# Both parts of a norm's operand at one place modulo 512 bytes

## The reference, cut to what matters

```python
def first_block(x, p, w_in, ...):
    for i in range(DEPTH):
        h = mixer_block(h, norm_mix[i], w_in[i], ...)   # rmsnorm(h) @ w_in, retention, gated delta rule
        u = rmsnorm(h, norm_ffn[i])
        if i % 2 == 0:
            h = h + swiglu(u, ffn_w_gate[j], ffn_w_up[j], ffn_w_down[j])
        else:
            h = h + moe(u, router[j], exp_w_gate[j], exp_w_up[j], exp_w_down[j])
        h = h + jax.nn.sigmoid(rmsnorm(h, norm_ple[i]) @ w_ple_gate[i]) * (p[i] @ w_ple[i])

def second_block(x, norm1_g, w_in, ...):
    for l in range(DEPTH):
        h = rmsnorm_2(x, norm1_g[l])
        u = jnp.einsum('btd,de->bte', h, w_in[l])       # then mLSTM, attention and HGRN side by side
        x = x + jnp.einsum('bte,ed->btd', mix, w_out[l])
        a = jnp.square(jax.nn.relu(jnp.einsum('btd,df->btf', rmsnorm_2(x, norm2_g[l]), w_up[l])))
        x = x + jnp.einsum('btf,fd->btd', a, w_down[l])
```

## Time and profile before

| | |
|---|---|
| median of three runs | 2189.08 us |
| profiled execution | 2186.53 us, span 2184.7 us |
| TensorE (PE) busy | 2111.8 us, 97%, 15466 products |
| its weight loads (PEld) busy | 1968.9 us, 90% |
| VectorE (DVE) busy | 1530.4 us, 70% |
| ScalarE (ACT) busy | 1366.6 us, 63% |
| mean granted TensorE clock | 0.989 of full speed |
| moved by DMA | 400.68 MB, mean 183 GB/s |

### The profile page before, as it was taken

How to read it: one execution, slowest core, us unless ns; L and a number is a source line. 1 busy time by engine, 2 the same in 40 slices (tenths; PEclk the granted TensorE clock), 3 DMA queues, 4 the chain that set the end, 5 groups by cost and what they waited for, 6 DMA issues and landing times.

```text
span 2184.7 us, 37308 instructions
## 1 busy us (share of the span) xinstructions
PE 2111.8 (97%) x15466; PEld 1968.9 (90%) x15466; DVE 1530.4 (70%) x2189; ACT 1366.6 (63%) x1884; POOL 65.4 (3%) x102
## 2 busy tenths in 40 slices
PE   8999999999999989997999999999989999999999
PEld 7988999999989889997888888888879999988999
DVE  5777456666567774563889999976868665876664
ACT  6765575544558655754877777776765545775553
POOL 0003000000000030000000000000000000000000
PEclk9999999999999999997999999999999999999999
DMA  7434345656554343452999999954416665523654
GB/s 260 153 118 125 94 144 183 189 175 192 166 170 142 118 124 102 136 188 108 332 330 336 327 324 329 341 210 146 141 39 178 189 193 164 161 68 121 196 186 135
DMA packets 126449, 400.68 MB, mean 183 GB/s; under 512 B 26048, under 2 KB 26432, under 8 KB 126272
## 3 DMA queue, kind: packets, MB, share of 16 engines
q1 hardware_dynamic: 126272, 398.20, 54.9%
HBM read 395.79 MB, written 2.36 MB: 182 GB/s over the span
## 4 chain that ended last, share of the span: by engine, by line
PE 84%; DVE 6%; ACT 6%; POOL 2%; issue 2%; DMA 0%; SPq 0%; DVEq 0%; ACTq 0%; POOLq 0%
PE ps L485 82%; DVE wlo L2136 2%; ACT whi L1383 1%; ACT scr L1393 1%; ACT arena L1393 1%; DVE arena L2136 1%; DVE arena L2144 1%; DVE scr L2136 1%; POOL arena L3087 1%; POOL arena L3090 1%; ACT L1393 1%; ACT L1387 0%; ACT rst L1393 0%; PE ps L1069 0%; DVE h L2136 0%
## 5 line engine op out<-in xcount | busy, mean ns | idle before, releaser
L2136 DVE TENSOR_TENSOR wlo<-raw,whi 128x1024 fp32r<-128x1024 f32 (+2 forms) x622 | 746.9, 1213 | 298.8 <-ACT whi L1383 293.3
L1383 ACT ACTIVATE whi<-raw 128x1024 fp32r<-128x1024 f32 (+2 forms) x622 | 643.2, 1042 | 317.4 <-PE ps L485 310.2
L485 PE MATMUL ps<-uh,whi 128*128 128x256 f32 x2240 | 646.1, 288 | 11.6 <-DVE arena L2144 3.9
L485 PE MATMUL ps<-uh,wlo 128*128 128x256 f32 x2240 | 631.5, 282 | 0.0
L485 PE MATMUL ps<-ul,whi 128*128 128x256 f32 x2240 | 625.0, 279 | 0.0
L485 PE MATMUL ps<-arena_r,whi 128*128 128x256 f32 x2720 | 475.7, 280 | 7.2 <-DVE arena_r L2136 6.3
L485 PEld LDWEIGHTS ps<-uh,whi 128*128 128x128 f32 x2240 | 419.3, 187 | 24.5 <-issue 13.2
L485 PEld LDWEIGHTS ps<-ul,whi 128*128 128x128 f32 x2240 | 421.1, 188 | 5.7 <-issue 5.3
L485 PEld LDWEIGHTS ps<-arena_r,whi 128*128 128x128 f32 x2720 | 414.4, 189 | 11.4 <-issue 7.8
L485 PEld LDWEIGHTS ps<-uh,wlo 128*128 128x128 f32 x2240 | 418.6, 187 | 0.0
L485 PE MATMUL ps<-arena_r,wlo 128*128 128x256 f32 x1360 | 377.9, 278 | 0.0
(11 more groups left out here) (175 smaller groups left out, 2241.3 us busy)
## 6 DMA issues: line engine op xcount, KB each, us to landing
raw<-stream SPq DMA_DIRECT2D x586, 512.0 KB, 4.2
arena<-stream SPq DMA_DIRECT2D x64, 512.0 KB, 5.6
CO<-stream SPq DMA_DIRECT2D x44, 512.0 KB, 5.5
raw<-stream SPq DMA_DIRECT2D x32, 384.0 KB, 4.7
arena<-stream SPq DMA_DIRECT2D x20, 384.0 KB, 4.4
CO<-stream SPq DMA_DIRECT2D x12, 384.0 KB, 4.5
CO<-const SPq DMA_DIRECT2D x2, 704.5 KB, 5.9
h<-xT SPq DMA_DIRECT2D x4, 256.0 KB, 5.7
```

Of the source, the lines that this page charges most:

```text
L485: return self.e.matmul(o, l, r, start=start, stop=stop, skip_group_check=True)
L1383: self.e.activation(M.whi[:, b:b + n], M.raw[a][:, 0:n], ACT.Copy).then_inc(K.sem("weight_hi"), 1)
L2136: return self.e.tensor_tensor(o, a, b, op)
```

## The change

uh and ul are allotted 2048 + 128 words in place of 2048 + 32, that is 8704 bytes each in place of 8320. What is given out of them is as before, OFF and STEP included. Everything behind them in the partition moves by 384 bytes (ul) or 768 bytes (scr, rst, eps, flag, the arena). UG's two tensors in the arena lose OFF and STEP: they are dense, 2048 words each, and start at word 4096 + 112 of the arena; HT, which follows them, starts at word 8304 in place of 8272. `Tiles.columns` is folded into the indexing. No instruction is added or taken away.

```diff
+LINE = 128
...
+        if k == ALL:
+            return Tiles(self.ap, c0, c1)
         if isinstance(k, slice):
...
-    def columns(self, c0, c1):
-        return Tiles(self.ap, c0, c1)
...
-        self.h, uh, ul = sb("h", 2048), sb("uh", 2048 + 2 * OFF, F32R), sb("ul", 2048 + 2 * OFF, F32R)
+        self.h, uh, ul = sb("h", 2048), sb("uh", 2048 + LINE, F32R), sb("ul", 2048 + LINE, F32R)
...
-        at = 4096 + OFF
-        self.UG = [[Tiles(ARr[:, at + i * (2048 + 2 * OFF):at + (i + 1) * (2048 + 2 * OFF)]) for i in range(2)], self.U]
-        at += 2 * (2048 + 2 * OFF)
+        at = 4096 + LINE - OFF
+        self.UG = [[v3(ARr[:, at + i * 2048:at + (i + 1) * 2048]) for i in range(2)], self.U]
+        at += 4096
...
-        ug = [x.columns(e % 2 * P, e % 2 * P + P) for x in self.M.UG[e // 2 % 2]]
+        ug = [x[:, :, e % 2 * P:e % 2 * P + P] for x in self.M.UG[e // 2 % 2]]
```

## The result

| | before | after |
|---|---|---|
| median of 6 runs each | 2189.52 us | 2198.19 us |
| lowest to highest | 2185.65 to 2195.08 | 2194.34 to 2199.04 |
| profiled execution | 2186.53 us, span 2184.7 | 2199.04 us, span 2197.3 |
| mean granted clock | 0.989 | 0.986 |

The ratio of after to before is 1.0032, 95% interval 1.0022 to 1.0042. That is a real loss of 8.7 us, under the 0.5% that the prediction called a change, and outside its range of 2152 to 2193.

The account below looks back on a forecast made before the run. TensorE's product spacing was taken as the bound. U's tight pace -30.9, tile 7 +8.4 and U off the path or loose after stalls +2.8 gave -19.7 us, so 2167 us; range 2152 to 2193 leaving out the slower case.

Parts of the forecast that it names:

- What bounds the kernel: Whole kernel: TensorE busy 2111.8 of 2184.7 us, so time is the number of products times their start-to-start spacing.
- So 64 keeps the tight pace: Arena-to-U hand-overs: uh's first product at 64 still takes 276 ns; the next, ul at 192, takes 281.
- The step at tile 7 brings a loose stream into it: U's last tile: its 32-byte shift makes the stream tight; with ul at 64, U's 6,720 products were to gain 30.9 us.
- Tile 7's price: U's tile 7 in 280 groups of 24: shifting a tight stream costs 0 to +8.4 us; +8.4 was taken.
- No gain: U's products: the step throws tight streams out as ul does; 2186.5 us if loose throughout, about 2176 if alternating; chance 0.11.
- The arena at 0, bounds +14.5 and -4: Arena's 4,080 moving products: going from 320 to 64 changes nothing, 0 us; bounds +14.5 all loose, -4 all tight.
- The experts at 0, bounds of 5.5: Experts' 1,104 products with UG or HT stationary: placement taken as 0 us, bounds -5.5 to +5.5 from 5 ns each way.
- a DMA share of 0.92: Experts' stretches: with DMA share at 0.92, running faster than now was hardly to be had.
- The sum: Whole kernel: -30.9 + 8.4 + 2.8 = -19.7 us, so 2166.8 us for the profiled execution, put at 2167.
- The second leg of *Slower: U and arena: 64 is a bad place; U stays at 118.0, arena falls to it, +14.5, 2201 us; whole rival 0.11.
- down groups of 22.6 us: Second block's feed-forward, down projection on the arena: growing from 21.77 us to this would show 64 a bad place.
- Place means nothing: U's streams: pace is set by the moment a stream starts, not operand placement; time stays 2186.5 us; chance 0.06.

Follow-up runs that it names:

- the kernel with two unlike tiles: Changed kernel with ul's tile 6 at 192 and tile 7 at 224, uh's at 64 and 96, the other tiles all at 64: 2174.55 us, 0.9930 to the kernel before.
- the alternation alone: Changed kernel without the 32-byte step, uh at 64 throughout, ul at 64 in tiles 0 to 3 and 192 in 4 to 7: 2195.75 us, 1.0024.
- one unlike tile: Changed kernel with ul's tile 6 at 192 beside uh's at 64, both parts' tile 7 at 96: 2188.09 us, 0.9998 to the kernel before.

## Why the prediction was wrong, step by step

- **What bounds the kernel** held: only the spacing of products moved the time.
- **"So 64 keeps the tight pace"** held, with alike parts too. A place where the changed kernel's U comes in tight, in order of time:

```profile
388.28 0.28 PE L485 MATMUL ps<-uh,whi 128*128 128x256 f32 x1
388.39 0.28 PE L485 MATMUL ps<-ul,whi 128*128 128x256 f32 x1
388.50 0.28 PE L485 MATMUL ps<-uh,wlo 128*128 128x256 f32 x1
...
389.52 0.28 PE L485 MATMUL ps<-uh,wlo 128*128 128x256 f32 x1
```

  From 388.28 to 389.52 are 11 spacings of 113 ns. In the earlier trace rows ul at 192 broke the pace at the second product; at 64 it does not. That 192 throws the stream out is borne out as well, by tile 6 in the kernel with two unlike tiles.

- **"The step at tile 7 brings a loose stream into it"** is the step that failed, and the forecast's whole gain rested on it. In the changed kernel 186 stall-free passages lead from loose to loose (176 inside U, 10 into the arena). The hand-over at 527 us, in order of time, answers to the earlier trace rows:

```profile
527.00 0.28 PE L485 MATMUL ps<-uh,whi 128*128 128x256 f32 x1
527.12 0.29 PE L485 MATMUL ps<-ul,whi 128*128 128x256 f32 x1
527.24 0.28 PE L485 MATMUL ps<-uh,wlo 128*128 128x256 f32 x1
527.36 0.40 PE L485 MATMUL ps<-arena_r,whi 128*128 128x256 f32 x2
527.60 0.28 PE L485 MATMUL ps<-arena_r,wlo 128*128 128x256 f32 x1
...
527.95 0.28 PE L485 MATMUL ps<-arena_r,wlo 128*128 128x256 f32 x1
```

  Tile 7 takes 0.36 us, much as before, but three arena products then take 0.35 where they took 0.33. The ten turns in the trace of before each had two things ahead of them, the step, and U's products with parts 128 bytes apart. I named the one and took the other for pure harm; the change removed it. The runs separate them: alternation and step turn the stream, the step alone does not (after), nor the alternation alone.

- **Tile 7's price** was bounded at 0 to 0.03 us a group for a tight stream. It is larger: the step ends the tight pace. All eight groups of the changed kernel that come to tile 7 tight have 117 to 119 ns on it; without the step fifteen of fifteen keep 113 there. A case in the changed kernel, in order of time:

```profile
793.00 0.28 PE L485 MATMUL ps<-uh,whi 128*128 128x256 f32 x1
793.11 0.28 PE L485 MATMUL ps<-ul,whi 128*128 128x256 f32 x1
793.22 0.28 PE L485 MATMUL ps<-uh,wlo 128*128 128x256 f32 x1
793.34 0.28 PE L485 MATMUL ps<-uh,whi 128*128 128x256 f32 x1
...
793.69 0.28 PE L485 MATMUL ps<-uh,whi 128*128 128x256 f32 x1
...
794.40 0.28 PE L485 MATMUL ps<-uh,whi 128*128 128x256 f32 x1
```

  Three products take 0.34 us up to tile 7, 0.35 on it, and behind it six take 0.71: the stream stays loose. This is half of the rival *No gain*, which had 0.11: its argument that "both could be enough" to throw U out was right. The other half, that the step is why U is loose, was not, since U stays loose without it.

- **The arena at 0, bounds +14.5 and -4**: measured +12.6, near the upper bound. The row it was taken from, uh at 64 in a tight stream, could only show that 64 keeps a pace, not that something would still turn the arena to it.
- **The experts at 0, bounds of 5.5**: measured -5.2. The estimate was read from a row of 384-column products, which did gain 2 ns (175.6 to 173.5). The 512-column ones, nearly five times as many, gained 5.3. That a DMA share of 0.92 would leave hardly anything to gain there did not hold: the whole kernel got 4.2 us faster by this part alone.
- **The sum.** U and its tile 7 were to give -22.5 us and gave -0.6; the arena, at 0, gave +12.6; the experts, at 0, gave -5.2. The first is the failed step, the second the same step seen from the arena, the third a term of its own that was too small.
- **The rivals.** The second leg of *Slower* (U stays at 118, the arena falls to it, 2201) is within 3 us of the time, but by another cause: its place 64 is harmless, as the arena loose at 320 and tight at 64 show. So the sign that the prediction named for it, down groups of 22.6 us, came, and would have led to the wrong cause. *Place means nothing* falls with the last table.

Why these two paces exist is open. The Trainium skill, "TensorE: Matmul & The Clock Gate", section "Back-to-back issue gap", gives N / 2.4 + 2.5 ns for an isolated product at full clock, an estimate of 109.2 for 256 columns; the tight pace, 113.3, is the nearest that a run here shows, and the loose one lies 8.6 above the estimate. The Trainium skill's "SBUF — State Buffer", section "Operand start alignment", treats where an operand starts as a matter of what is legal and says that its runs "timed nothing"; here the place of the experts' stationary operands was worth 5 ns a product.

## What to carry to other kernels

When a stream has two paces at one address, ask of each turn in the trace what the good turns have in common, all of it, before a part is taken away as harm: here an irregular layout paid for its own cost by what it did to the operand after it. Test such a rule on both halves (the alternation without the step, the step without the alternation) before the layout is made regular. Of the versions here, the one to keep has two unlike tiles: once tight, it holds the pace over 18 of 24 products, and it gives the arena its turn.

## What the runs showed of the hardware that was not expected

- The pace of a stream of products depends on what went before it, and lasts: 113.3 or 117.8 ns for the same shape, same clock and same addresses.
- A loose stream turned tight after at least one tile's alternation by 128 bytes, then a step of 32 bytes, and then parts alike; with a step of 64 bytes in its place, or none, it turned in none of 345 passages inside U. Without any alternation it turned in none of 345 either, with the step (176) or without (169).
- The rule does not say when. With one unlike tile every third group of a long run was tight, though the two loose groups between differed by only 0.01 us.
- With two unlike tiles a stream that had been tight over tiles 0 to 5 was tight again behind tile 7 in 119 of 123 passages, a loose one in 29 of 64, into the arena included. So more decides than the six loose products between. What holds this memory no run here shows.
- Stationary operands of the experts with both parts at 0 modulo 512 bytes: 227.4 ns for 512 columns; 232.7 with both at 128, or at 384 and 0.
